# Second layer of a hybrid decoder: retention, state update, recurrence, head norms and small transposes gathered into one block

## Chip, cores and metric

The kernel runs on one core of one Trainium2 chip. The metric is the device time of one execution in microseconds (us); lower is better. Several runs of a kernel are timed, and one execution is recorded by the hardware profiler.

## The reference

One inference step of a two-layer decoder: a prompt of 16 meta and 512 prompt tokens (528 columns here) and eight sequences of four new tokens (32 columns), so T = 560 columns in all. The change lies in the mixer of the second layer, which joins a RetNet retention (four heads of 128) and a gated recurrence (RG-LRU, width 512):

```python
def retention_chunk(S, seqs):
    ...
    intra = jnp.einsum('bhts,bhsv->bhtv', jnp.einsum('bhtd,bhsd->bhts', q, k) * D, v)
    inter = jnp.einsum('bhtd,bhdv->bhtv', q, S) * jnp.exp((t + 1.0)[None, :] * lg[:, None])[None, :, :, None]
    ...
    S_new = jnp.exp(L * lg)[None, :, None, None] * S + jnp.einsum('bhsd,hs,bhsv->bhdv', k, w_src, v)
    return S_new, intra + inter

def mixer_odd(...):
    ...
    mu = jnp.mean(hr, axis=-1, keepdims=True)
    var = jnp.mean(jnp.square(hr - mu), axis=-1, keepdims=True)
    hr = (hr - mu) * lax.rsqrt(var + EPS) * ret_ln_g.astype(f32)[None, :, None, :]
    hr = jax.nn.silu(rg.astype(f32)) * from_heads(hr)
    ...
    r = jax.nn.sigmoid(...)
    ig = jax.nn.sigmoid(...)
    log_a = -LRU_C * r * jax.nn.softplus(-lru_lambda.astype(f32))
    a = jnp.exp(log_a)
    bx = jnp.sqrt(-jnp.expm1(2.0 * log_a)) * (ig * xc)
    bx = bx.at[:, 0].add(a[:, 0] * h0)
    _, hs = lax.associative_scan(_lin_combine, (a, bx), axis=1)
    hl = hs * jax.nn.gelu(lgate.astype(f32))
    out = jnp.concatenate([hr, hl], axis=-1).astype(xn.dtype) @ w_out
    return out, S_new, hs[:, -1], u[:, -(CONV_W - 1):]
```

The new retention states, the last recurrence values and the last three convolution inputs are outputs as well.

## The kernel before

Activations lie transposed, features on the 128 partitions and the 560 columns along the free axis. Each engine has its own queue and runs it strictly in the order in which the kernel writes it; engines meet at semaphores. Code is written in blocks (`nc.Block()`): a block has one section per engine, and at its end all engines meet in a barrier before the next block begins.

The first layer and the second layer's input projection come first. Then the mixer of the second layer runs in four blocks, one after the other, and after them `close_layer(1, ...)` runs the output projection, the norms and the feed-forward network.

Block 1, `decayed_attention` (L1075 on). Four heads with eight tiles each (the list `ALL`; within a head the tiles are 256, 128, 272, 272, 272, 144, 16 and 32 columns wide). TensorE first runs four products of the all-ones tile with itself (`warm(3)`, L460). Then, for tile i, it writes the scores of tile i+1 (L1092) and adds tile i's weighted values to the head's sums (L1116). Between the two VectorE multiplies the scores by the decay table (L1199, "weights" here). A head's last tile also adds the decode sequences' old states (eight products of 4 columns, L1134). ScalarE copies the sums out of PSUM (L1158, L1161), a head at a time. At the start ScalarE also makes the small lambda columns (with GpSimd), then Silu of `rg` and Gelu of `lgate` (L3084, L3085). SyncE loads the old states.

Block 2, `state_update` (L1312 on). VectorE scales the values of each block of keys by its decay (L1334, with a column copy L1336 that only the first layer needs) and spreads the 32 sample rows over eight sequences (L1341, eight instructions a head). TensorE multiplies them by the keys (L1377, L1381); VectorE adds the sums to the decayed states (L1351; L1360, eight instructions a head). Beside it TensorE makes the recurrence's eight gates (L3110), ScalarE their Sigmoid (L3127), then Tanh and Exp (L3132, L3135), GpSimd the product of input gate and input (L3141). At the end VectorE makes 1 - a squared (L3146).

Block 3 (L3186 on). SyncE stores the new states. TensorE sums each head with the all-ones matrix (L3209), VectorE subtracts the mean (L3231), ScalarE squares (L3264), TensorE sums the squares with one column per head (L3200), VectorE takes 1/(var + eps) (L3236, L3239), ScalarE the root (L3268), TensorE spreads the row over the partitions (L3220), VectorE multiplies (L3247) and GpSimd multiplies by the gate (L3277). In the same queues stand the recurrence's decay (L3261), its root (L3266), inputs (L3171), the four sample steps (L3177, L3179), the four scans over the prompt (L3184, one per 128 channels) and the product with Gelu (L3274). Last VectorE gathers the small rows (L3252 to L3256).

Block 4, `transposes` (L485): the small rows are turned by TensorE, copied (L493, L499) and stored by SyncE (L3291 to L3295); the block ends when the stores have landed.

The order of the work around the change is thus the order of the code in each queue; nothing plans it.

## Time and profile before

| | us |
|---|---|
| median of 3 runs (lowest to highest) | 1703.52 (1691.70 to 1703.73) |
| the profiled execution | 1702.52 |
| its span on the core | 1700.9 |
| mean granted TensorE clock of the span | 0.945 of full speed |
| busy, TensorE / VectorE / ScalarE / GpSimd | 1569.6 / 1022.2 / 619.4 / 293.8 |

Times in the trace count from the span's start. The stage that is changed begins at 1111.2 with the first instruction after a barrier and ends at 1229.6 with the output projection's first product. PE is TensorE, DVE VectorE, ACT ScalarE, POOL GpSimd, SPq SyncE's DMA queue.
### The profile page before, as it was taken

The numbers are of one execution on the slowest core, as the hardware profiler recorded it, in microseconds if no ns is written. First come the engines' busy times: TensorE is split into PE (matmuls) and PEld (weight loads), VectorE is DVE, ScalarE is ACT, GpSimd is POOL, SyncE is SP. The second block draws the span as 40 slices with busy tenths as digits, with TensorE's granted clock in tenths as the row PEclk, the third lists the DMA queues.
The fourth block names the chain that finished last, engine by engine and source line by source line (L and its number), as shares of the span: only waits on it lengthen the run. The fifth ranks groups of instructions, "written<-read, shape, count | busy, mean of one in ns | idle before, by whom it ended". The sixth has DMA issues, their size and how long they took to land. (4 is left out here: it accounts for less than half of the span.)

```text
span 1700.9 us, 31137 instructions
## 1 busy us (share of the span) xinstructions
PE 1569.6 (92%) x11877; PEld 1459.3 (86%) x11877; DVE 1022.2 (60%) x1761; ACT 619.4 (36%) x1073; POOL 293.8 (17%) x304
## 2 busy tenths in 40 slices
PE   7999989988889999999999899998498999999996
PEld 5999966766578999999999899975298999999996
DVE  5332454544556988888322867427658988885225
ACT  3111322435334435556122422224234345555221
POOL 2411001300000154443000100001300344441000
PEclk8999987979999999999999999988599999999998
DMA  5232151777351123333332132211130323325311
GB/s 141 78 100 62 50 163 38 230 217 251 96 163 50 50 76 99 99 99 103 92 99 66 50 99 98 87 50 46 49 112 1 99 76 99 99 80 131 93 43 53
DMA packets 225861, 161.15 MB, mean 95 GB/s; under 512 B 17949, under 2 KB 206089, under 8 KB 225760
## 3 DMA queue, kind: packets, MB, share of 16 engines
q1 hardware_dynamic: 222480, 157.94, 32.1%
q0 software_dynamic: 3280, 1.85, 0.5%
q8 instruction: 66, 1.08, 0.3%
q14 instruction: 35, 0.29, 0.1%
HBM read 150.13 MB, written 9.89 MB: 94 GB/s over the span
## 5 line engine op out<-in xcount | busy, mean ns | idle before, releaser
L2315 ACT CAST w_high<-ring 128x1024 fp32r<-128x1024 f32 (+1 forms) x68 | 81.5, 1199 | 345.2 <-PE psum L2045 317.8
L2149 PE MATMUL psum<-t_high,piece_high 128*128 128x280 f32 (+1 forms) x512 | 150.0, 293 | 10.2 <-ACT product L2460 7.5
L2625 DVE TENSOR_TENSOR w_low<-ring,w_high 128x1024 fp32r<-128x1024 f32 (+1 forms) x68 | 96.0, 1412 | 100.2 <-ACT w_high L2315 100.2
L2151 PE MATMUL psum<-t_high,piece_low 128*128 128x280 f32 (+1 forms) x512 | 149.4, 292 | 0.0
L2150 PE MATMUL psum<-t_low,piece_high 128*128 128x280 f32 (+1 forms) x512 | 149.2, 291 | 0.0
L2415 ACT CAST piece_high<-ring 128x512 fp32r<-128x512 f32 x160 | 99.1, 622 | 76.6 <-PE psum L2151 55.0
L2149 PE MATMUL psum<-b_high,piece_high 128*128 128x280 f32 (+1 forms) x384 | 112.5, 293 | 0.0
L2151 PE MATMUL psum<-b_high,piece_low 128*128 128x280 f32 (+1 forms) x384 | 112.4, 293 | 0.0
L2150 PE MATMUL psum<-b_low,piece_high 128*128 128x280 f32 (+1 forms) x384 | 112.2, 292 | 0.0
L2149 PEld LDWEIGHTS psum<-t_high,piece_high 128*128 128x128 f32 x512 | 97.4, 190 | 11.1 <-ACT product L2460 7.9
L2150 PEld LDWEIGHTS psum<-t_low,piece_high 128*128 128x128 f32 x512 | 97.5, 190 | 0.0
L2151 PEld LDWEIGHTS psum<-t_high,piece_low 128*128 128x128 f32 x512 | 97.3, 190 | 0.0
L343 PE MATMUL psum<-normed_high,w_high 128*128 128x280 f32 x448 | 94.3, 292 | 0.6 <-PEq L530 0.6
L2740 DVE TENSOR_TENSOR piece_low<-ring,piece_high 128x512 fp32r<-128x512 f32 x96 | 92.8, 970 | 1.8 <-ACT piece_high L2415 1.6
L343 PE MATMUL psum<-normed_high,w_low 128*128 128x280 f32 x448 | 93.8, 290 | 0.0
L343 PE MATMUL psum<-normed_low,w_high 128*128 128x280 f32 x448 | 93.5, 290 | 0.0
L2045 PE MATMUL psum<-hidden_high_a,w_high 128*128 128x280 f32 (+1 forms) x308 | 89.3, 290 | 0.0
L2045 PE MATMUL psum<-hidden_high_b,w_high 128*128 128x280 f32 (+1 forms) x308 | 89.2, 290 | 0.0
L2045 PE MATMUL psum<-hidden_low_b,w_high 128*128 128x280 f32 (+1 forms) x308 | 89.1, 289 | 0.0
L2045 PE MATMUL psum<-hidden_high_a,w_low 128*128 128x280 f32 (+1 forms) x308 | 89.1, 289 | 0.0
L2045 PE MATMUL psum<-hidden_low_a,w_high 128*128 128x280 f32 (+1 forms) x308 | 89.1, 289 | 0.0
L2045 PE MATMUL psum<-hidden_high_b,w_low 128*128 128x280 f32 (+1 forms) x308 | 89.0, 289 | 0.0
(541 smaller groups left out, 4613.6 us busy)
## 6 DMA issues: line engine op xcount, KB each, us to landing
ring<-in_ffn_wd SPq DMA_DIRECT2D x16, 1408.0 KB, 7.0
ring<-in_ffn_wg SPq DMA_DIRECT2D x40, 512.0 KB, 4.0
ring<-in_ffn_wu SPq DMA_DIRECT2D x40, 512.0 KB, 5.2
ring<-in_w_in_even SPq DMA_DIRECT2D x14, 1024.0 KB, 5.3
ring<-in_w_in_odd SPq DMA_DIRECT2D x12, 1024.0 KB, 5.1
ring<-in_cache_fox_k SPq DMA_DIRECT2D x44, 256.0 KB, 4.2
projected<-in_cache_fox_v SPq DMA_DIRECT2D x28, 256.0 KB, 3.2
projected<-in_cache_fox_k SPq DMA_DIRECT2D x20, 256.0 KB, 4.2
```

Of the source, the lines that this page charges most:

```text
L343: last = nc.tensor.matmul(banks[2 * tl + half][:, 0:HALF], w[:, k, :], m[:, half * HALF:(half + 1) * HALF], start=(kk == 0 and w is w_high ...
L2045: done = mm(banks[2 * tl + a][:, 0:HF], w, m[a], start=first and s == 0, stop=last and s == 2)
L2149: mm(bank, wh[:, k], xh[:, k, :], start=(j in (0, 1, 3) and k == 0), stop=False, skip_group_check=True)
L2150: mm(bank, wh[:, k], xl[:, k, :], start=False, stop=False, skip_group_check=True)
L2151: last = mm(bank, wl[:, k], xh[:, k, :], start=False, stop=(k == 3), skip_group_check=True)
L2315: nc.scalar.copy(dst, src).then_inc(w_hi[p], 1)
L2415: nc.scalar.copy(dst, chunks(src, 4) if j in (0, 1, 5) else src).then_inc(pc_high, 1)
L2625: v.tensor_tensor(dst, src, high_.bitcast(F32), ALU.subtract).then_inc(w_lo[p], 1)
L2740: last = v.tensor_tensor(chunks(pc_l[j][:, :], 4), chunks(src, 4), chunks(pc_h[j][:, :], 4).bitcast(F32), ALU.subtract)
```

## The change

The four blocks become one. Nothing of the first layer changes but the place from which some semaphores are taken (`decode_sem` in place of `sem`, which frees them after the first layer). In the new block:

- The four warm-up products are gone; TensorE begins with the first two gates. Gates 2 to 6 follow tiles 3 to 7, gate 7 tile 9. The transposes of the convolution rows stand after tile 18.
- Each head's weighted sums get their own pair of banks by the parity of the head, so the next head does not wait for the copy.
- Between the tiles' weights VectorE scales the sources of the first two heads, and from tile 18 on does the recurrence: 1 - a squared after tiles 18 to 21, the inputs after 24 to 27, the sample steps after tile 29, scans 0 and 1 after tiles 30 and 31, scans 2 and 3 between the head norms.
- Centring is a product: TensorE multiplies a head by (identity - 1/128) (`centre`). ScalarE squares that product out of PSUM, and VectorE multiplies it by `rg` in one step. `rg` has been through Silu and has been multiplied by the norm's gain on GpSimd. The last step is one product with the spread root.
- The spreading of sample rows is one instruction of 1024 elements per head in place of eight; adding to the states is two of 512 in place of eight of 128; the column copies are gone.
- The final row gathering is on GpSimd. SyncE stores the convolution rows early and the new states when all four heads are updated; the block ends when all stores have landed.

The core of the diff (the loops that set the order; the waits are shown where the prediction speaks of them):

```diff
-    decayed_attention(rq, rk, TK["mv"], Cst, bufs, False, dtab, dsm[:, :, 0:NS],
-                      lambda_by_scalar, lambda_by_gpsimd, None, load_ret_state, s_st2)
-    state_update(TK["mk"], TK["mv"], Cst, lambda n, b, hd: dsm[0:n, hd, 2 * NS + b:2 * NS + b + 1],
...
-    transposes(jobs, store_lru)
+        def _(sp):
+            load_ret_state(sp)
+            sp.wait_ge(rows_copied, 2)
...
+            sp.wait_ge(rows_copied, 4)
...
+            sp.wait_ge(state_done, MH)
+            for b in range(NB):
+                sp.dma_start(io["s_ret_S"][b].rearrange("h k v -> k h v"),
...
+            sp.wait_ge(stored, 16 * 16)
...
+            for i in range(len(ALL)):
+                if i + 1 < len(ALL):
+                    score(i + 1)
+                values(i)
+                if 3 <= i <= 7:
+                    lru_gate(i - 1)
+                if i == 9:
+                    lru_gate(7)
+                if i == 18:
+                    turn_conv()
+                if i == 26:
+                    centred_head(0)
+                if i == 30:
+                    centred_head(1)
+            centred_head(2)
+            update(0)
+            centred_head(3)
+            update(1)
+            for hd in range(MH):
+                variance(hd)
+            update(2)
+            update(3)
+            turn_fin()
+            for hd in range(MH):
+                spread_rstd(hd)
...
+            for c in range(4):
+                nc.scalar.activation(gt[:, c, :], ga[:, c, :], ACT.Tanh, scale=lam[:, 2, c:c + 1]).then_inc(tanh_done, 1)
+            for i in range(2):
+                act.wait_ge(rows_turned, i + 1)
+                n = (3, 24)[i]
+                nc.scalar.copy(crow[i][0:n, :], banks[i][0:n, :]).then_inc(rows_copied, 1)
+            for c in range(4):
+                nc.scalar.activation(hs[:, c, :], ga[:, c, :], ACT.Exp, scale=lam[:, 0, c:c + 1]).then_inc(a2_done, 1)
+            copied(1)
...
+            def one_minus_a2(c):
+                dve.wait_ge(tanh_done, c + 1)
+                dve.wait_ge(a2_done, c + 1)
...
+            def recurrence_input(c):
+                dve.wait_ge(root_done, c + 1)
...
+            for i in range(len(ALL)):
+                weights(i)
+                if i % 8 < 5 and i < 16:
+                    source_block(i // 8, i % 8)
...
+                if 18 <= i < 22:
+                    one_minus_a2(i - 18)
+                if 24 <= i < 28:
+                    recurrence_input(i - 24)
+                if i == 28:
+                    scaled_head(0)
+                if i == 29:
+                    sample_steps()
+                if i >= 30:
+                    scan(i - 30)
+            scaled_head(1)
+            scan(2)
+            scaled_head(2)
+            state(0)
+            scan(3)
+            scaled_head(3)
+            sources(2)
+            state(1)
+            sources(3)
+            dve.wait_ge(variances, MH)
...
+            v.reciprocal(vrow, vrow).then_inc(inverted, 1)
+            state(2)
+            state(3)
```

Three places show how the queues change. The first is TensorE's queue where the stage begins; `ones` is the all-ones tile, `convolved` the gates' input. Before:

```order
L460 MATMUL psum<-ones 128x512 x4
L1092 MATMUL psum<-projected 128x256
L1092 MATMUL psum<-projected 128x128
L1116 MATMUL psum<-projected,token_major_6482 128x256
L1092 MATMUL psum<-projected 128x272
L1116 MATMUL psum<-spare,token_major_6482 128x128
L1092 MATMUL psum<-projected 128x272
L1116 MATMUL psum<-projected,token_major_6482 128x272
```

and after:

```order
L3165 MATMUL psum<-convolved,projected 128x280 x4
L3136 MATMUL psum<-projected 128x256
L3136 MATMUL psum<-projected 128x128
L3148 MATMUL psum<-projected,token_major_6480 128x256
L3136 MATMUL psum<-projected 128x272
L3148 MATMUL psum<-projected,token_major_6480 128x128
L3136 MATMUL psum<-projected 128x272
L3148 MATMUL psum<-projected,token_major_6480 128x272
L3136 MATMUL psum<-projected 128x272
L3148 MATMUL psum<-projected,token_major_6480 128x272
L3165 MATMUL psum<-convolved,projected 128x280 x2
L3136 MATMUL psum<-projected 128x144
```

Two gates (four products of 280 columns) stand where the warm-up stood, and single gates come between tiles from tile 3 on.

The second is ScalarE's queue from the gates' Tanh on (`root` takes it; `rstd` is the row of the norm). Before, in blocks 2 and 3:

```order
L3132 ACTIVATE root<-input_gate,lam 128x560 x4
L3135 ACT_TABLE_LOAD
L3135 ACTIVATE projected<-input_gate,lam 128x560 x4
L1326 UNCONDITIONAL_BRANCH
L3258 UNCONDITIONAL_BRANCH
L3261 ACTIVATE input_gate<-input_gate,lam 128x560 x4
L3264 ACTIVATE token_major_6482<-projected 128x560 x4
L3266 ACT_TABLE_LOAD
L3266 ACTIVATE root<-root 128x560 x4
L3268 ACTIVATE rstd<-rstd 4x560
```

and after:

```order
L3302 ACTIVATE root<-input_gate,lam 128x560 x4
L3306 COPY projected<-psum 3x512
L3306 COPY projected<-psum 24x512
L3308 ACT_TABLE_LOAD
L3308 ACTIVATE recurrent<-input_gate,lam 128x560 x4
L3272 COPY projected<-psum 128x256
L3272 COPY projected<-psum 128x304
L3312 ACTIVATE input_gate<-input_gate,lam 128x560 x4
L3313 ACT_TABLE_LOAD
L3313 ACTIVATE projected<-projected 128x2240
L3316 ACT_TABLE_LOAD
L3316 ACTIVATE root<-root 128x560 x4
```

The copies of the turned convolution rows (L3306) now stand between Tanh and the Exp of a squared; Silu of `rg` (L3313) stands between the decay and the root (L3316).

The third is VectorE's queue in the third head of the retention, tiles 16 on; `decay_table` is the factor of a tile's weights. Before:

```order
L1199 TENSOR_TENSOR projected<-psum,decay_table_6485 128x256
L1199 TENSOR_TENSOR spare<-psum,decay_table_6485 128x128
L1199 TENSOR_TENSOR projected<-psum,decay_table_6485 128x272
L1199 TENSOR_TENSOR spare<-psum,decay_table_6485 128x272
L1199 TENSOR_TENSOR projected<-psum,decay_table_6485 128x272
L1199 TENSOR_TENSOR spare<-psum,decay_table_6485 128x144
L1199 TENSOR_TENSOR projected<-psum,decay_table_6485 16x16
L1199 TENSOR_TENSOR spare<-psum,dsm 32x32
```

and after:

```order
L3340 TENSOR_TENSOR projected<-psum,decay_table_6483 128x256
L3340 TENSOR_TENSOR projected<-psum,decay_table_6483 128x128
L3340 TENSOR_TENSOR projected<-psum,decay_table_6483 128x272
L3372 SCALAR_TENSOR_TENSOR root<-recurrent,root 128x560
L3340 TENSOR_TENSOR projected<-psum,decay_table_6483 128x272
L3372 SCALAR_TENSOR_TENSOR root<-recurrent,root 128x560
L3340 TENSOR_TENSOR projected<-psum,decay_table_6483 128x272
L3372 SCALAR_TENSOR_TENSOR root<-recurrent,root 128x560
L3340 TENSOR_TENSOR projected<-psum,decay_table_6483 128x144
L3372 SCALAR_TENSOR_TENSOR root<-recurrent,root 128x560
```

After tile 18's weights an instruction of the recurrence (L3372, 1 - a squared) follows each tile's weights, ahead of those of the next tile.

## Rows read from the trace of the kernel before

**Rows 1.** Windows: stretch, length, busy PE, PEld, DVE, ACT, POOL, granted clock, DMA share, GB/s.
```profile
1111.10:1116.40 5.30, 5.23 (x9) 2.25 (x10) 0.00 (x0) 5.13 (x7) 1.33 (x6) 0.68 0.71 206
...
1116.40:1152.60 36.20, 35.79 (x193) 28.43 (x191) 10.66 (x32) 7.45 (x11) 0.00 (x0) 0.91 0.10 28
...
1182.90:1219.60 36.70, 18.93 (x48) 9.92 (x48) 25.00 (x48) 9.70 (x14) 13.39 (x8) 0.64 0.23 65
```

**Rows 2.** Timeline, TensorE, retention: start, length, engine, line, what, count.
```profile
1111.17 5.37 PE L460 MATMUL psum<-ones 128*128 128x512 f32 x8 [2.20 <-PEq L124]
...
1116.37 0.82 PE L1092 MATMUL psum<-projected 128*128 128x256 f32 x4
...
1133.28 1.95 PE L1134 MATMUL psum<-qs,states 128*128 128x4 f32 x16
...
1137.76 1.11 PE L1116 MATMUL psum<-projected,token_major 128*128 128x272 f32 x2
...
1142.96 1.95 PE L1134 MATMUL psum<-qs,states 128*128 128x4 f32 x16
...
1150.54 1.95 PE L1134 MATMUL psum<-qs,states 128*128 128x4 f32 x16
```

**Rows 3.** Timeline, TensorE: two gates, four products of 280 columns.
```profile
1162.16 2.15 PE L3110 MATMUL psum<-convolved,projected 128*128 128x280 f32 x8
```

**Rows 4.** Instructions by line, ScalarE, in the stage: busy time, mean ns of one.
```profile
L3132 ACT ACTIVATE root<-input_gate,lam 128x560 f32<-128x560 f32 x4 | 2.7, 750 | 0.1
...
L3135 ACT ACT_TABLE_LOAD x1 | 1.3, 1283 | 0.1
...
L3084 ACT ACTIVATE projected<-projected 128x2240 f32<-128x2240 f32 x1 | 2.1, 2070 | 0.0
...
L3266 ACT ACTIVATE root<-root 128x560 f32<-128x560 f32 x4 | 2.3, 657 | 0.0
...
L1158 ACT COPY projected<-psum 128x256 f32<-128x256 f32 (+1 forms) x6 | 2.3, 389 | 21.9 <-PE psum L1134 18.6 <-PE psum L1116 3.4
```

**Rows 5.** Instructions by line, VectorE, from the state update to the end.
```profile
L3171 DVE TENSOR_TENSOR spare<-spare,root 128x560 f32<-128x560 f32 x4 | 2.6, 707 | 0.0
...
L3184 DVE TENSOR_TENSOR_SCAN recurrent<-input_gate,spare 128x528 f32<-128x528 f32 x4 | 6.9, 1797 | 0.1
...
L3231 DVE SCALAR_TENSOR_TENSOR projected<-psum,projected 128x280 f32<-128x280 f32 x8 | 3.2, 444 | 6.5 <-PE psum L3209 6.5
...
L1360 DVE SCALAR_TENSOR_TENSOR states<-states,psum 128x128 f32<-128x128 f32 x32 | 6.6, 277 | 0.0
...
L3239 DVE RECIPROCAL rstd<-rstd 4x560 f32<-4x560 f32 x1 | 3.6, 3641 | 0.1
...
L3179 DVE TENSOR_TENSOR recurrent<-recurrent,spare 128x32 f32<-128x32 f32 x4 | 0.9, 218 | 0.3
```

**Rows 6.** Timeline, VectorE and GpSimd, with and without each other.
```profile
1154.83 1.65 DVE L1341 TENSOR_SCALAR projected<-token_major,mwbuf 32x128 f32<-32x128 f32 x8
...
1157.99 3.97 DVE L1341 TENSOR_SCALAR projected<-token_major,mwbuf 32x128 f32<-32x128 f32 x8
...
1158.03 1.37 POOL L3141 TENSOR_TENSOR spare<-spare,convolved 128x560 f32<-128x560 f32 x1 [42.37 <-ACT spare L3127]
...
1205.09 8.10 POOL L3274 TENSOR_TENSOR projected<-recurrent,projected 128x560 f32<-128x560 f32 x4 [30.82 <-DVE recurrent L3184]
```

**Rows 7.** Timeline and waits, state stores and entry to the output projection.
```profile
1182.91 5.95 SPq L3190 DMA_DIRECT2D out_s_ret_S<-states  x8
...
1188.90 0.88 SPq L3192 DMA_DIRECT2D out_p_ret_S<-cp  x1
...
SPq L3186 <- DMA out_p_ret_S<-cp: 2.8, 1, 2.8
...
1226.54 0.41 SPq L1972 DMA_DIRECT2D first_w<-in_ffn_wg  x1
...
1229.64 0.79 PE L2045 MATMUL psum<-mixed_high,w_high 128*128 128x272 f32 x2 [7.71 <-DVE mixed_low L2633]
```

More of the change, by code:

```diff
@@ new lines, in hybrid_decoder @@
+    crow = [flat(lx)[0:24, 1024 + 512 * i:1536 + 512 * i] for i in range(2)]
+    vrow = rstd[0:4, :]
+    halves = [slice(0, HALF), slice(HALF, T)]
+    own = smask[:, 32:40]
+    (scored, weighted, weights_used, num_copied, centre_made, centred, scaled, squared, variances, inverted, rooted, spread,
+     head_done) = (sem(x) for x in (
+         "scores", "weights", "weights_used", "num_copied", "centre_matrix", "centred", "centred_scaled", "centred_squared",
+         "variances", "variances_inverted", "rstd_rows", "rstd_spread", "head_done"))
@@ new lines, in centred_head @@
+            def centred_head(hd):
+                if hd == 0:
+                    pe.wait_ge(centre_made, 1)
+                    pe.wait_ge(rows_copied, 2)
+                elif hd == 2:
+                    pe.wait_ge(num_copied, 8)
+                else:
+                    pe.wait_ge(scaled, hd)
+                    pe.wait_ge(squared, hd)
+                pe.wait_ge(num_copied, 2 * hd + 2)
+                for half in range(2):
+                    last = mm(centre_banks(hd)[half][:, 0:HALF], centre, xn[:, hd, halves[half]], start=True, stop=True)
+                last.then_inc(centred, 1)
@@ new lines, in variance, with update @@
+                last.then_inc(variances, 1)
+            def update(hd):
+                pe.wait_ge(sourced, hd + 1)
+                if hd == 0:
+                    pe.wait_ge(scaled, 2)
+                    pe.wait_ge(squared, 2)
+                    pe.wait_ge(weighted, len(ALL))
+                elif hd == 1:
+                    pe.wait_ge(num_copied, 6)
+                else:
+                    pe.wait_ge(state_done, hd - 1)
+                for b in range(SB):
+                    n = BLK[b][1]
+                    mm(sum_bank(hd)[:, 0:128], TK["mk"][0:n, b, hd * 128:(hd + 1) * 128], vw[hd % 2][0:n, b, :],
+                       start=(b == 0), stop=(b == SB - 1))
+                ks = TK["mk"][0:NS, SB, hd * 128:(hd + 1) * 128]
+                for half in range(2):
+                    last = mm(sequence_banks(hd)[half][:, :], ks,
+                              vm[hd % 2][:, 4 * half:4 * half + 4, :].rearrange("p b v -> p (b v)"), start=True, stop=True)
+                last.then_inc(updated, 1)
@@ new lines, in scan, with scaled_head @@
+            def scan(c):
+                v.tensor_tensor_scan(hs[:, c, 0:TP], ga[:, c, 0:TP], gi[:, c, 0:TP], 0.0, ALU.mult, ALU.add).then_inc(scanned, 1)
+            def scaled_head(hd):
+                dve.wait_ge(squared, hd + 1)
+                dve.wait_ge(gain_rg, hd + 1)
+                for half in range(2):
+                    last = v.tensor_tensor(xn[:, hd, halves[half]], centre_banks(hd)[half][:, 0:HALF], rg[:, hd, halves[half]],
+                                           ALU.mult)
+                last.then_inc(scaled, 1)
@@ new lines, in state @@
+            def state(hd):
+                dve.wait_ge(updated, hd + 1)
+                v.tensor_copy(cp[:, hd, 0:128], sum_bank(hd)[:, 0:128])
+                st = states[:, :].rearrange("p (b h v) -> p b h v", b=NB, h=MH)
+                for half in range(2):
+                    x = st[:, 4 * half:4 * half + 4, hd, :]
+                    last = v.scalar_tensor_tensor(out=x, in0=x, scalar=GAMMA4[hd],
+                                                  in1=sequence_banks(hd)[half].rearrange("p (b v) -> p b v", b=4),
+                                                  op0=ALU.mult, op1=ALU.add)
+                last.then_inc(state_done, 1)
@@ L3251, in _ @@
[L3251 to L3268 removed]
+                    c = halves[half]
```

415 lines of the change are left out of this document (233 added, 182 removed).

## Prediction

> **What bounds the kernel now.** I read the windows first, to find a stage in which TensorE is not the limit; then the timeline of that stage engine by engine, for what each engine waits on; then the instructions by line, for prices. The windows show the stage [rows 1]: during the retention (1116.4 to 1152.6) TensorE is busy throughout and VectorE for 10.7 of 36.2 us; in the third block (1182.9 to 1219.6) TensorE is busy for 18.9 of 36.7 us at a mean granted clock of 0.64, and VectorE for 25.0. So the stage has a part in which TensorE works and the others are idle, and a part in which they work in a chain and TensorE waits. It runs from 1111.17, the warm-up products [rows 2], to 1229.64, the first product of the output projection [rows 7]: 118.5 us. Everything before and after is unchanged, so I put the new block's work on the same clock and ask when that first product starts.
>
> **The change, step by step.** Each step follows the engine that is late.
>
> (a) *To the end of the convolution transposes after tile 18* (call it Y): TensorE is late. Before, the first score stood at 1116.37 and tile 18 of the third head ended at 1138.87 (1137.76 + 1.11): 22.5 us for 19 tiles [rows 2]. That now begins 5.2 us earlier, at 1111.17. Added in front of Y are eight gates. Two gates take 2.15 us with the latency of the last product [rows 3], so some 0.95 each: 7.6 us. Eight transposes of 128 columns move 1024 columns; at the rate of [rows 3], about 590 columns per us of fp32 product they take at most 1.7, I take 1.5. The first 5.3 us had a granted clock of 0.68 [rows 1], and useful work now lies in them: 0.32 x 5.3 = 1.7 us lost. Against that the gates fill waits: heads two and three end with the state products 9.7 us apart (1133.28, 1142.96), head four 7.6 us later (1150.54), for the same work [rows 2]. Of these twice 2.1 us I give 2.0 back. Y = 1111.2 + 22.5 + 7.6 + 1.5 + 1.7 - 2.0 = 1142.5. VectorE's scaled sources, which now stand between the tiles, cost 0.21 each at the rate of the first line of [rows 6], one per tile of about 0.9 us or more: hidden by TensorE; not hidden, twelve of them would be 2.5 us.
>
> (b) *From Y to the first root*: ScalarE is late. It stands at the copies of the transposed rows, so its Exp can't begin before Y, although the Tanh is long done; and 1 - a squared, which waits for that Exp, stands in VectorE's queue ahead of tile 19's weights, so TensorE waits for VectorE and VectorE for ScalarE. ScalarE then runs [rows 4]: two copies 0.8, table load 1.28, four Exp 2.7, two copies 0.8, four Exp 2.7, table load 1.28, Silu 2.07, table load 1.28, first root 0.6: 13.5, with handoffs 14.0. First root at 1156.5. TensorE's tiles 19 to 24 are less than this and lie beside it.
>
> (c) *To tile 28's weights*: VectorE is late. Four recurrence inputs 2.6 (L3171 in [rows 5]) and the weights of tiles 25, 26, 27 between them (128 and twice 272 columns; a product of 280 out of PSUM takes 0.40 by L3231, 3.2 over 8): 1.2. 1160.3.
>
> (d) *To the end of the retention* (t0): VectorE again. Weights 28 0.4; head 0's product with `rg` 0.8 (two of L3231's size); weights 29 0.3; eight sample steps at 0.29 (0.22 of L3179 and a drain) 2.3; weights 30 0.2; scan 1.74 (L3184, 6.9 over 4); weights 31 0.2: 5.9, with handoffs 6.3. TensorE ends with a tile and eight state products, 2.3. t0 = 1168.9. Before, this was 1152.5: the retention itself becomes longer, because it takes the others' work into its queues.
>
> (e) *To the last head's states*: ScalarE's copy 0.4 and square 0.9 come first, then VectorE is late: three products with `rg` 2.4, two scans 3.5, four state updates, two sources, the variance row 0.8 (two of 280 columns, as L3231) and the reciprocal 3.64 [rows 5]. A state update was a copy and eight instructions, 6.6 / 4 = 1.65 for the eight; two instructions over the same elements lie between twice the 0.66 of L3171's 560 columns, scaled to 512, that is 1.2, and 1.65; with the copy I take 1.5, four are 6.0. The sources: five scalings and a small one 1.3, and one instruction of 1024 elements, between 1.2 (1024/560 of 0.66) and the 1.65 of the first line of [rows 6]; I take 1.2, since one instruction is nearest the 560-column row; twice 2.5 is 5.0. Sum 21.3, and 0.4 waiting for TensorE's first update. TensorE's own work here, about 17 us at 590 columns per us (four updates of 1664 columns, four variance pairs, two centrings), is shorter and lies beside it. t0 + 23.0 = 1191.9.
>
> (f) *The stores.* The eight state stores wait for the last head; issue to landing was 1182.91 to 1188.90 + 0.88 + 2.8 = 1192.6: 9.7 us [rows 7]. Before, norms and recurrence lay beside them; now only the last norm products (four spread pairs and four products of 0.8) do, and the block's end waits for the stores: 1201.6. The small rows' stores stand ahead of them in SyncE's queue, and end at about the same time as the last state update; if they are late, the stores are late with them.
>
> (g) *Entry*: from the first DMA of the next block to the first product 3.1 us [rows 7], and I allow 0.4 from landing to that DMA: 1205.1.
>
> Saved: 1229.64 - 1205.1 = 24.5 us. From the profiled execution's 1702.52 (its span is 1700.9, 1.6 less; it lies 1.0 under the median of the runs shown) that leaves 1678. What goes by name: the warm-up, three barriers, the third block's chain (Exp, root, inputs, scans one after the other) and the last transposes with their stores; what comes back is a longer retention and stores with nothing left beside them.
>
> Not shown by the trace: GpSimd's product of `rg` with a column. Its nearest row is 1.37 (L3141, same 560 columns, two tiles) and for an operation at the same engine 2.03 at most (8.10 over 4) [rows 6]; it is needed at (d), some 5 us after Silu, and hidden either way.
>
> **A rule against the change.** In [rows 6] eight VectorE scalings take 1.65 alone and 3.97 beside two GpSimd products, 1.16 more for each product. The scans, with two inputs in SBUF, kept 1.74 each, while GpSimd's products beside them rose from 1.37 to 2.03. The Trainium skill, page "SBUF — State Buffer", section "Who interferes with whom", says that a VectorE instruction with two SBUF inputs, or a scaling or copy in a two-port mode, and a GpSimd instruction that reads SBUF exclude each other, and that the one that starts later waits. The trace agrees for the scalings, and in the scans it was GpSimd that lost. By that rule the recurrence inputs of (c) could each be held by a product of `rg` with its gain, 4 x 1.37 = 5.5 us, and the time would be 1683.5; the GpSimd rival below holds that and more.
>
> **Rivals.** *GpSimd holds VectorE.* Twelve GpSimd products stand beside VectorE work that is now on the path (four with the input gate, four with the gain, four with Gelu). At 1.16 us each [rows 6] that is 13.9 us: 1692. For it: VectorE is late in (c) to (e). Against: most products out of PSUM have one SBUF input, and the Gelu products are held back until the last score.
>
> *The clock and the waits are kinder.* If TensorE gets its full clock after the start and the gates fill every wait, Y comes after 19 tiles at head four's pace (19/8 x 7.6 = 18.1), 7.6 gates, 1.0 transposes and 1.7: 1139.6; and with updates and sources at their lower bounds (1.2 less in (e)) the time is 1674.
>
> *The clock stays low; slower than before.* Every wait of TensorE that (b) and (d) introduce is a pause after which it may run at 1.2 GHz, as the third block shows (0.64) [rows 1]. At half clock throughout, (a)'s 28 us of work at full speed (18.1 + 7.6 + 1.5) double and Y comes at 1166, 24 later; in (e) TensorE's 17 us become 34 against VectorE's 23, 11 later: 1713, so 35 lost against 24.5 saved. It decides where the mean granted clock of the block falls under about 0.6; the retention before had 0.91 [rows 1], and its queue was no fuller than the new one. The Trainium skill, page "TensorE: Matmul & The Clock Gate", section "HAM oscillation — how this bites in real kernels", describes that: bursts divided by waits begin throttled each time. By that rule the waits of (b) would bring on this rival in part.
>
> **How the numbers follow.** Forecast 0.55, kinder 0.22, GpSimd 0.18, low clock 0.05. The likeliest gives 1678. The range holds the first three: from 1662 (the kinder case, less the 12 us by which the lowest run before lies under the median) to 1695 (the GpSimd case, with 3 us for its own handoffs). One per cent of 1703.5, about what a measurement can tell from no change, is 17 us, so faster by over 1% means under 1686.5: forecast (0.53 of 0.55), kinder, and little of the GpSimd case (0.03): 0.78. Within 1%: the rest of these and most of the low-clock case: 0.19. Slower by over 1%: 0.03.
>
> **What would show it.** In the new trace: the first gate at the block's start and no warm-up; the first wait of (b), VectorE idle after tile 18's weights for ScalarE's Exp, some 3 us, and again before the first input for the root; VectorE's weights 28 to 31 spread over 6 us; the retention's last product near 1169; state stores issued near 1192 with SyncE's last wait on them; the output projection's first product near 1205. Wrong would be: a granted clock under 0.7 between tiles 19 and 31; VectorE scalings or inputs of twice their length beside GpSimd; stores issued well before the last norm product of 0.8 us has run, with the end set by the norms; or a time outside the stage that moves.

## The result, and the profile after

The changed kernel takes 1678.8 us, the median of four runs (1674.0 to 1684.1), against 1703.6 for the kernel before (1691.7 to 1705.1): a ratio of 0.988, with a 95% interval of 0.985 to 0.992, which is some 20 us; the medians themselves lie 24.8 us apart. Timed once more beside other runs it took 1680.2 against 1703.4, a ratio of 0.986 (0.982 to 0.990). The profiled execution took 1684.14 us, the longest of the first four.

Whole times move by 5 us and more from one execution to the next, largely ahead of the stage: in the fourteen profiled executions of this study, whose programs are the same up to there, the stage began anywhere from 1102.7 to 1115.9 us. Behind the stage thirteen of them took 469.7 to 472.2 us, and one, the run with the warm-up put back, 467.1. So below, the stage itself is what is compared, from its first product to the output projection's first product, each time in the clock of its own trace. It was 118.5 us before [rows 2, 7]. After, in TensorE's timeline (start, length, line, names, shape, count, and the idle time before):

```profile
1112.40 2.89 PE L3165 MATMUL psum<-convolved,projected 128*128 128x280 f32 x8 [2.03 <-PEq L124]
...
1211.59 0.79 PE L2045 MATMUL psum<-mixed_high,w_high 128*128 128x272 f32 x2 [7.67 <-DVE mixed_low L2633]
```

1211.59 - 1112.40 = 99.2 us: the stage is 19.3 us shorter, where 24.5 had been forecast. Its windows, cut at the points of the prediction's steps (transposes after tile 18, first root, end of the retention, last state); the columns are those of [rows 1], the number behind POOL being the granted clock:

```profile
1112.30:1145.20 32.90, 32.62 (x151) 25.77 (x152) 12.32 (x34) 15.11 (x29) 8.59 (x18) 0.84 0.24 64
1145.20:1158.50 13.30, 9.78 (x36) 7.28 (x35) 4.46 (x10) 13.13 (x18) 1.79 (x2) 0.60 0.02 5
1158.50:1174.70 16.20, 14.14 (x56) 11.20 (x55) 9.89 (x23) 6.65 (x11) 9.17 (x7) 0.71 0.00 1
1174.70:1198.40 23.70, 21.85 (x86) 12.28 (x86) 19.92 (x38) 4.67 (x11) 3.21 (x5) 0.92 0.01 1
1198.40:1211.60 13.20, 5.50 (x13) 3.51 (x13) 5.17 (x11) 3.10 (x5) 0.00 (x0) 0.52 0.78 219
```

Two things stand there. TensorE is busy in the first stretch for 32.6 of 32.9 us and in the fourth for 21.9 of 23.7: what lay behind the retention does lie beside it now. Over the whole stage, before and after:

```profile
1111.10:1229.60 118.50, 85.18 (x346) 56.15 (x346) 65.60 (x201) 41.53 (x64) 20.32 (x18) 0.78 0.15 43
```
```profile
1112.30:1211.60 99.30, 83.90 (x339) 60.05 (x339) 51.76 (x115) 42.66 (x71) 22.76 (x31) 0.76 0.19 51
```

TensorE's busy time and clock are nearly the same; its waiting fell from 33.3 to 15.4 us, which is 17.9 of the 19.3 us saved.

The second thing is the granted clock, 0.91 in the retention before [rows 1]. It is 0.84, then 0.60 and 0.71, between the clock's two levels. In the first stretch it is low at the start and again ahead of the end of the transposes, and there TensorE is busy without a break:

```profile
1112.30:1116.70 4.40, 4.21 (x13) 3.10 (x13) 0.81 (x3) 4.21 (x6) 1.15 (x6) 0.65 0.69 201
...
1138.00:1145.20 7.20, 7.20 (x29) 5.87 (x29) 0.73 (x2) 0.42 (x1) 0.00 (x0) 0.56 0.00 0
```

ScalarE's timeline shows who is late after tile 18, and VectorE's who waits for it:

```profile
1132.90 2.72 ACT L3302 ACTIVATE root<-input_gate,lam 128x560 f32<-128x560 f32 x4
1144.78 1.05 ACT L3306 COPY projected<-psum 3x512 f32<-3x512 f32 x2 [9.16 <-PE psum L3174]
...
1147.14 2.72 ACT L3308 ACTIVATE recurrent<-input_gate,lam 128x560 f32<-128x560 f32 x4
...
1157.92 2.35 ACT L3316 ACTIVATE root<-root 128x560 f32<-128x560 f32 x4
```
```profile
1148.01 0.74 DVE L3372 SCALAR_TENSOR_TENSOR root<-recurrent,root 128x560 f32<-128x560 f32 x1 [5.62 <-ACT recurrent L3308]
...
1158.62 1.08 DVE L3378 TENSOR_TENSOR spare<-spare,root 128x560 f32<-128x560 f32 x1 [3.46 <-ACT root L3316]
...
1167.88 1.24 DVE L3393 TENSOR_TENSOR_SCAN recurrent<-input_gate,spare 128x528 f32<-128x528 f32 x1
```

ScalarE has its Tanh done at 1135.6 (1132.90 + 2.72) and stands for 9.16 us at the copies of the turned rows, L3306, until TensorE has turned them; the Exp, L3308, comes after. VectorE waits 5.62 us for that Exp and 3.46 for the first root, the two waits that the prediction named (the first as some 3 us). At the end, SyncE's queue:

```profile
1198.40 5.96 SPq L3122 DMA_DIRECT2D out_s_ret_S<-states  x8
...
1208.48 0.38 SPq L1972 DMA_DIRECT2D first_w<-in_ffn_wg  x1
```

The stores go out as the last state is done, and the next block's first DMA follows 10.1 us after their first issue, long after the last norm product (1203.96 + 0.80, VectorE).

This table is worked out from the traces, as microseconds after the stage's first product. "First root" is the start of the first Sqrt; for the forecast that is its first root at 45.3 less the 0.6 that the root takes.

| kernel | transposes end | first root | retention ends | last state | next block's product | median, us |
|---|---|---|---|---|---|---|
| forecast | 31.3 | 44.7 | 57.7 | 80.7 | 93.9 | 1678 |
| changed | 32.8 | 45.5 | 62.3 | 86.0 | 99.2 | 1678.8 |
| changed, again | 32.8 | 45.5 | 62.3 | 86.0 | 99.2 | 1680.2 |
| a1 Exp first | 32.8 | 38.1 | 54.3 | 78.5 | 91.7 | 1675.7 |
| a2 warm-up back | 33.6 | 46.4 | 62.8 | 93.1 | 107.2 | 1682.5 |
| a3 stores by head | 32.8 | 45.5 | 62.3 | 86.0 | 95.7 | 1680.2 |
| a4 gain left out | 33.1 | 45.8 | 62.7 | 86.4 | 99.6 | (1678.6, one run) |
| a5 gates first | 40.0 | 52.7 | 68.8 | 92.7 | 106.0 | 1689.5 |
| a6 unread products | 33.1 | 45.8 | 59.3 | 83.0 | 96.2 | (1685.3, one run) |
| a7 = a1 and a3 | 33.1 | 38.5 | 54.7 | 78.8 | 89.6 | 1668.7 |
| a8 = a7 and products | 29.9 | 36.5 | 50.8 | 76.6 | 86.8 | 1669.0 |

The ratios to the kernel before, with their intervals: a1 0.986 (0.979 to 0.993), a2 0.988 (0.982 to 0.995), a3 0.989 (0.982 to 0.995), a5 0.992 (0.989 to 0.996), a7 0.982 (0.978 to 0.986), a8 0.979 (0.975 to 0.982). The intervals of a1, a2, a3 and a5, and at its edge that of a7, overlap the changed kernel's, so by whole times they can't be told from it with certainty; what is read below from the stages rests on one execution each. Of the six runs of a8 each is faster than every one of the changed kernel timed beside them (1664.4 to 1671.1 against 1676.8 to 1684.6).

### The profile page after: what moved, and what is told of

Its sections match the earlier page's. It is cut to its first block and busy times, and to the rows that moved or that the text cites. A ratio compares the mean times of both kernels' runs of the same rounds, so it can differ in the third digit from the quotient of the medians.

```text
span 1682.5 us, 31038 instructions
## 1 busy us (share of the span) xinstructions
PE 1570.8 (93%) x11869; PEld 1464.0 (87%) x11869; DVE 1009.5 (60%) x1675; ACT 620.4 (37%) x1080; POOL 297.5 (18%) x317
```

## The experiments

**The same kernel again**, with no edit.

> The changed kernel once more, with nothing edited. Theory (the stage repeats itself, and the spread of the whole time comes from the clock in the first layer, ahead of the stage): transposes 32.8 to 33.1, end of the retention 62.3, last state 86.0 and first product of the output projection 99.2 after the first gate, each within 1 us, whatever the whole time is. Rival (the clock varies in the stage itself, as in the run with the warm-up, where the part after the retention took 30.3 instead of 23.7): the stage lies anywhere from 96 to 106.

All five points came back to within 0.1 us, though the whole time of that execution was 1678.4 instead of 1684.1. Its stretches, cut as above, show the same clock too:

```profile
1139.60:1152.90 13.30, 9.77 (x36) 7.30 (x34) 4.46 (x10) 13.13 (x18) 1.82 (x2) 0.59 0.02 5
1152.90:1169.10 16.20, 14.13 (x56) 11.19 (x55) 9.91 (x23) 6.62 (x11) 9.14 (x7) 0.71 0.00 1
1169.10:1192.80 23.70, 21.83 (x86) 12.26 (x86) 19.92 (x38) 4.67 (x11) 3.20 (x5) 0.92 0.01 1
```

So the low clock in it is no accident of one execution. But the stage does not repeat in every one: of the eight traces in which TensorE's work up to the transposes is the same, seven end them at 32.8 to 33.1 us and one, the last experiment's, at 29.9, at another clock. A difference of a microsecond may be read from one trace here where it lies in the step that the edit touches; one that comes with another clock elsewhere may be that of one execution.

**ScalarE's copies behind the Exps.**

```diff
-            for i in range(2):
-                act.wait_ge(rows_turned, i + 1)
...
             for c in range(4):
                 nc.scalar.activation(ga[:, c, :], ga[:, c, :], ACT.Exp, scale=lam[:, 3, c:c + 1]).then_inc(a_done, 1)
+            for i in range(2):
+                act.wait_ge(rows_turned, i + 1)
+                n = (3, 24)[i]
+                nc.scalar.copy(crow[i][0:n, :], banks[i][0:n, :]).then_inc(rows_copied, 1)
```

> The changed kernel, with ScalarE's two copies of the turned convolution rows moved behind both sets of Exp. Theory (ScalarE is late from the transposes to the first root, because it stands at these copies from 1135.6 to 1144.8 with its Tanh done): the Exp of a squared runs right after the Tanh, VectorE's wait of 5.6 us for it and its wait of 3.5 us for the root go, and the stage from the first gate to the first product of the output projection falls from 99.2 to 92 to 94 us. Rival (TensorE is late there: it is busy 9.8 of these 13.3 us at a granted clock of 0.60): the waits go over to TensorE's products, and the stage falls by 0 to 3.5 us.

The stage is 91.7 us, 7.5 less, a little more than the theory had. The transposes end at the same 32.8, so all of it comes from step (b) and stays to the end. The trace of this run, TensorE and then ScalarE:

```profile
1106.69 2.90 PE L3165 MATMUL psum<-convolved,projected 128*128 128x280 f32 x8 [2.03 <-PEq L124]
...
1143.33 1.95 PE L3154 MATMUL psum<-qs,states 128*128 128x4 f32 x16
...
1198.42 0.79 PE L2045 MATMUL psum<-mixed_high,w_high 128*128 128x272 f32 x2 [6.66 <-DVE mixed_low L2633]
```
```profile
1131.22 2.72 ACT L3304 ACTIVATE recurrent<-input_gate,lam 128x560 f32<-128x560 f32 x4
...
1144.81 2.35 ACT L3316 ACTIVATE root<-root 128x560 f32<-128x560 f32 x4
```

The Exp now follows the Tanh, and the root comes 5.4 us after the transposes (1139.46) instead of 12.7. TensorE's tiles 19 to 24 keep up with that: they have no wait ahead of them and run at full clock, and head three's state products take 1.95 us at 1143.33 against 3.58 in the changed kernel. The rival had read TensorE's 9.8 busy microseconds as work that had to be done there; it was work at the low clock, with waits around it.

**The warm-up put back** (`warm(3)` ahead of the first gate).

> The changed kernel, with the four warm-up products back ahead of the first gate. Theory (the warm-up cost 5.4 us, and the real work that took its place lost 1.7 of them to the low clock): the first gate comes 5.4 us later and runs at full clock, the stage from the first of these products to the output projection is 99.2 + 3.4 to 5.0. Rival (what the warm-up saved was lost again to a low clock in the first gates and tiles): 99 to 100.5.

Neither. The stage is 107.2, 8.0 longer, but not for the reason given: with 5.2 us of warm-up ahead, the transposes end only 0.8 later. The windows tell why, and where the rest went:

```profile
1121.10:1149.60 28.50, 28.05 (x152) 22.05 (x151) 12.09 (x33) 10.77 (x23) 6.54 (x8) 1.00 0.12 32
...
1178.80:1209.10 30.30, 29.72 (x86) 15.54 (x86) 19.92 (x38) 4.78 (x11) 3.21 (x5) 0.66 0.00 0
```

Behind the warm-up TensorE has its full clock up to the transposes (1.00), where the changed kernel has 0.84: so leaving the warm-up out saved 5.2 us and gave back 4.4 of them here (32.8 against 28.4 from the first gate). In the last experiment below, also without warm-up, that part took 29.9 at 0.94, so what is given back differs between executions. The other 7 us are lost from the end of the retention to the last state, 30.3 us against 23.7, at a clock of 0.66 against 0.92, with TensorE busy for 29.7 of them. What sets the clock low in that stretch is open: TensorE was not waiting there. Nor is it shown to be the edit's doing: the profiled execution was the longest of the four (1691.8; the others 1678.4 to 1683.0), and their median lies only 2 to 4 us above the changed kernel's.

**The kernel before without its warm-up** (`warm(3)` in the first layer's retention only), one part of the change alone.

> The kernel before, without the four warm-up products ahead of the second layer's retention: one part of the change alone. Prediction's price (5.4 us, of which 1.7 are lost to the low clock): the stage of 118.5 falls to 114.5 to 115.5. Rival (by the run with the warm-up put back, in which the transposes came only 0.8 us later, the low clock takes nearly all of it back): 117 to 118.5.

```profile
1112.83 0.89 PE L1092 MATMUL psum<-projected 128*128 128x256 f32 x4 [2.20 <-PEq L124]
...
1228.14 0.79 PE L2046 MATMUL psum<-mixed_high,w_high 128*128 128x272 f32 x2 [7.72 <-DVE mixed_low L2634]
```

1228.14 - 1112.83 = 115.3: 3.2 us less, by the prediction's price. The median was 1699.1 against 1701.05 (ratio 0.999, 0.996 to 1.002), so by time alone it can't be told from nothing.

**The kernel before with the wider update instructions**, the other part that can be had alone. The short form of the edit, for the second layer:

```diff
-                    for b in range(NB):
-                        last = v.tensor_scalar(vm[hd % 2][:, b, :], ..., mw[:, b:b + 1], None, ALU.mult)
+                    last = v.tensor_tensor(vm[hd % 2][:, :, :], ..., mw.unsqueeze(2).to_broadcast([NS, NB, 128]), ALU.mult)
...
-                    for b in range(NB):
-                        s = state[:, b * MH + hd, :]
+                    for half in range(2):
+                        x = st[:, 4 * half:4 * half + 4, hd, :]
```

> The kernel before with the state update's wider instructions alone: one instead of eight for the scaled samples, two instead of eight for a head's states, and no copies of the weights. VectorE is busy for 27.0 of the second block's 30.3 us [rows 5 have its parts]. Theory (VectorE is late there, and what it loses is gained): 4 x 0.44 + 4 x 0.38 from the two lines alone and the copies, 1.4 twice, and the 3.97 of the scalings beside GpSimd: 5 to 7.5 us, a stage of 111 to 113.5. Rival (TensorE, busy for 22.9 of the 30.3, or ScalarE's gates are late next): 1 to 4 us, 114.5 to 117.5.

Below both: the stage is 119.3 (1105.99 to 1225.25), no shorter than before. VectorE's lines in the second block:

```profile
L1346 DVE TENSOR_TENSOR projected<-token_major,mwbuf 32x1024 f32<-32x1024 f32 x4 | 4.9, 1213 | 0.3
...
L1357 DVE COPY cp<-psum 128x128 f32<-128x128 f32 x4 | 1.2, 292 | 12.4 <-PE psum L1394 12.4
```

The scaled samples of a head take 1.21 us, as the prediction's bound had it, and VectorE's busy time in the block falls from 27.0 to 17.9. All of it comes back as 12.4 us of waiting for TensorE's update products (L1357), which stand in one queue with the gates, and these wait for ScalarE (0.97 us at a time). TensorE's clock in the block was 0.85, against 0.90 before, which may be part of why nothing was gained. In the old order shorter instructions were worth nothing; what they are worth in the new one no run shows. So of the 19.3 us the warm-up is some 3 (in the kernel before) and the wider instructions alone nothing; what is left, some 16, is the order of the work together with what was not tried alone: the centring as a product, the dropped barriers, and the wider instructions in the new order. That is by difference and not by a run of its own.

**All gates ahead of the first score.**

```diff
-            lru_gate(0)
-            lru_gate(1)
+            for i in range(8):
+                lru_gate(i)
```

> The changed kernel, with all eight gates ahead of the first score instead of between the tiles. Theory (the gates between the tiles fill waits of TensorE, which the prediction put at 2.0 us): the transposes after tile 18 come 2 us later and the stage is 100.5 to 101.5. Rival (TensorE has no such waits where the gates stand, or ScalarE's earlier Tanh gives them back): 98.5 to 99.5.

The direction is the theory's, the size is not: the transposes end 7.2 us later, the stage is 106.0. TensorE waits 3.38 us for ScalarE's first Sigmoid, which stands behind three table loads and the logarithm of lambda, and gets its eight gates done only at 1130.0, 15.8 us after the first:

```profile
1114.21 2.12 PE L3165 MATMUL psum<-convolved,projected 128*128 128x280 f32 x8 [2.03 <-PEq L124]
1119.72 8.15 PE L3165 MATMUL psum<-convolved,projected 128*128 128x280 f32 x20 [3.38 <-ACT input_gate L3275]
1128.84 1.21 PE L3165 MATMUL psum<-convolved,projected 128*128 128x280 f32 x4 [0.97 <-ACT input_gate L3275]
```

So the gates between the tiles hide ScalarE's pace. The theory's gaps of TensorE's own were not there (see step (a) below).

**Four unread products in each of TensorE's two waits.**

```diff
+                if i in (19, 30):
...
+                    for _ in range(4):
+                        mm(banks[0][:, 0:256], ones[:, :], ones[:, :].unsqueeze(1).to_broadcast([128, 2, 128]), start=True, stop=True)
                 values(i)
```

> The changed kernel with four products of 256 columns, whose results nobody reads, in each of TensorE's two waits of the retention (before tile 19's and tile 30's values). Theory (TensorE's waits bring the low clock on): the state products of heads three and four take 1.95 us each as they do at full clock instead of 3.58, the centring of head 1 some 1.1 instead of 2.2, the granted clock from the transposes to the end of the retention rises from 0.60 and 0.71 to over 0.85, and the stage falls from 99.2 to 95 to 97. Rival (the low clock comes whatever TensorE does there, as in the run with the warm-up, where it stood at 0.66 through 30 us of busy TensorE): these durations stay, and the stage is 99 to 100.

Half of each. The stage is 96.2, inside the theory's range, and all 3.0 us are gained between the first root and the end of the retention, where the clock is 0.87; from the transposes to the first root it is 0.74, and nothing is gained:

```profile
1157.41 3.58 PE L3154 MATMUL psum<-qs,states 128*128 128x4 f32 x16
...
1168.90 1.99 PE L3250 MATMUL psum<-ones 128*128 128x256 f32 x8
...
1172.76 1.95 PE L3154 MATMUL psum<-qs,states 128*128 128x4 f32 x16
```

After the second wait was filled, head four's state products take 1.95 us, at full clock; so they do in the last experiment, and in none of the traces without these products. After the first, head three's still take 3.58: the tile right behind it ran at full clock (0.73 us at 1152.46), the 256-column score at 1155.69 did not (1.22 against 0.70). That wait was filled in part only: 1.29 us of it were left behind the unread products.

**Stores head by head.**

```diff
-            sp.wait_ge(state_done, MH)
-            for b in range(NB):
-                sp.dma_start(io["s_ret_S"][b].rearrange("h k v -> k h v"), ...)
+            for hd in range(MH):
+                sp.wait_ge(state_done, hd + 1)
+                sp.dma_start(io["s_ret_S"][:, hd].rearrange("b k v -> k b v"), by_head[:, hd]).then_inc(stored, 16)
+                sp.dma_start(io["p_ret_S"][0, hd], cp[:, hd, 0:128]).then_inc(stored, 16)
```

> The changed kernel, with the states stored head by head as each is done, instead of sequence by sequence after the last. Theory (the 10.1 us from the last state to the next block's first DMA are the stores alone, with nothing beside them): the last head's store lands some 4 to 5 us after the last state, the block then ends with the last norm products (1204.8), and the stage falls from 99.2 to some 95.5 to 96.5. Rival (a store has a long fixed part from issue to landing, or the earlier stores slow the states or are slower in this shape): 98 to 100.

95.7, as the theory had it, with every point up to the last state where it was:

```profile
1197.29 0.39 SPq L3119 DMA_DIRECT2D out_s_ret_S<-states  x1
1197.72 0.58 SPq L3120 DMA_DIRECT2D out_p_ret_S<-cp  x1
1201.78 0.39 SPq L1972 DMA_DIRECT2D first_w<-in_ffn_wg  x1
```

The next block's DMA follows 4.5 us after the last head's store, 0.3 after the last norm product.

**GpSimd's gain left out.**

> The changed kernel with GpSimd's four products of the gate with the head gain cut to 8 of 560 columns (the rest of the gain is left out). Theory (GpSimd's products lengthen the four recurrence inputs beside them by 0.8 us in all, from 0.66 each to 1.08, 0.72, 0.73 and 0.92, and nothing more): these take 0.66 to 0.73 each and the stage is 98 to 98.8. Rival (each input is held by a product, 1.37 each, as the page's rule had it): 93 to 95.

```profile
1152.69 0.74 DVE L3378 TENSOR_TENSOR spare<-spare,root 128x560 f32<-128x560 f32 x1 [3.46 <-ACT root L3316]
...
1155.62 0.73 DVE L3378 TENSOR_TENSOR spare<-spare,root 128x560 f32<-128x560 f32 x1
```

The four inputs fall to 0.73 each, 2.9 in all instead of 3.45, and the stage doesn't change (99.6). From the first input to tile 28's weights it is 5.4 us, as in the changed kernel (5.3): VectorE now waits 0.82 and 0.72 us for the scores instead, the first of which TensorE gives at the low clock, while the second stands behind head 0's centring in its queue. The gain's products cost nothing there.

**The kernel before with GpSimd held back until the scans are done** (its wait for scan c + 1 made a wait for all four).

> The kernel before, with GpSimd's four products of the recurrence held back until all four scans are done. Theory (VectorE's scans were lengthened by the GpSimd products beside them, as 1.74 before against 1.24 in the changed kernel says): each scan takes 1.24, the four 5.0 instead of 6.9, and GpSimd's products fall from 2.03 to about 1.4. Rival (the prediction's reading, that it was GpSimd alone that lost): scans stay at 1.74.

```profile
1199.39 4.70 DVE L3184 TENSOR_TENSOR_SCAN recurrent<-input_gate,spare 128x528 f32<-128x528 f32 x4
```
```profile
1204.17 5.34 POOL L3274 TENSOR_TENSOR projected<-recurrent,projected 128x560 f32<-128x560 f32 x4 [34.56 <-DVE recurrent L3184]
```

Four scans in 4.7 instead of 6.9 [rows 5], four products in 5.3 instead of 8.1 [rows 6]: both had lost. It is a test of these durations only; the stage, with the products now behind the scans, got no shorter (120.2).

**Both gains together.**

> The changed kernel with both edits: ScalarE's copies behind the Exps, and the states stored head by head. Theory (the two lie one behind the other on the path, the first before the last state and the second after it): the stage is 91.7 less the 3.5 that the stores gave, some 88 to 89 us, and the time lies some 10 us under that of the changed kernel at the same clock in the first layer. Rival (with the states earlier, another wait takes over: the norm products or the clock): 90 to 92.

89.6, between the two: 9.6 of the 11.0 us that the edits gave one by one. The next DMA now leaves at 1189.20, right after the last norm product (1188.93), so the norm products are late in place of the stores, as the rival said.

**And the unread products with them.**

> The changed kernel with ScalarE's copies behind the Exps, the stores by head, and four unread products of 256 columns in TensorE's wait before tile 30's values (that wait alone: the other is gone with the first edit). Theory (the wait before tile 30 brings on the low clock for the end of the retention): the head's state products take 1.95 instead of 3.58 and the stage falls from 89.6 to 86.5 to 87.5. Rival (what the end of the retention gains is lost again behind it to VectorE or to the clock): 89 to 90.5.

86.8, and head four's state products do take the theory's 1.95 us, but the time was not gained by its path. The first stretch, which this edit doesn't touch, is 3.2 us shorter (29.9 instead of 33.1), at another clock:

```profile
1110.80:1140.70 29.90, 29.60 (x151) 23.30 (x152) 13.82 (x37) 21.00 (x38) 8.52 (x18) 0.94 0.26 71
...
1147.30:1161.60 14.30, 14.17 (x62) 10.50 (x61) 9.87 (x23) 7.22 (x11) 8.84 (x7) 0.81 0.00 1
1161.60:1187.40 25.80, 25.30 (x87) 13.83 (x86) 19.63 (x37) 4.78 (x11) 4.60 (x7) 0.79 0.19 54
```

From the transposes to the first root 1.3 us are lost (6.6 against 5.3), from there to the end of the retention 1.9 gained (14.3 against 16.3), and then 1.7 lost up to the last state (25.8 against 24.1, at 0.79 against 0.85) and 0.5 gained behind it. So the unread products' own gain is not shown to last. The time is that of the two edits alone as far as the measurement can tell (1669.0, 1668.7). Both medians lie some 10 us under the changed kernel's.

## Why the prediction was right, and where it was not

The time came out within 1 us of the forecast of 1678, inside the range, and by the medians faster by over 1% (the interval of the ratio reaches to 0.8%). The stage did not: it saved 19.3 us of the 24.5 forecast. The medians differ by 24.8, the two profiled executions by 18.4; the place of the stage in the trace moves by up to 13 us from run to run, so the 5 us between medians and stage need no cause in the kernel, and none is shown. The hit on the time is in part luck. Step by step, with the forecast ahead of the measured length:

- (a) 31.3, 32.8. TensorE is late there and busy throughout, as said. "Against that the gates fill waits", the 2.0 us given back, failed: there was no wait to fill. In the kernel before, heads two and four between the ends of their state products:

```profile
1125.55:1135.23 9.68, 9.68 (x49) 7.73 (x50) 2.69 (x8) 0.79 (x2) 0.00 (x0) 0.82 0.00 0
...
1144.91:1152.49 7.58, 7.58 (x47) 6.07 (x46) 2.26 (x7) 0.79 (x2) 0.00 (x0) 1.00 0.00 0
```

  TensorE is busy for all of both, so the 2.1 us that head two took longer are low clock (0.82 against 1.00) and not waiting; [rows 1] had it busy for 35.79 of 36.20 us. The 22.5 us for 19 tiles were themselves taken at 0.86 (1116.40 to 1138.87), so some 3.1 of them, as an estimate, are low clock (22.5 x 0.14). Without these and without the 2.0, the sum at full clock is 19.4 + 7.6 + 1.5 = 28.5; the run with the warm-up took 28.4 at 1.00. The 1.7 us for the start were right in size (4.4 us at 0.65, so 1.5 lost). Missing was a term for the second spell of low clock, 7.2 us at 0.56, so some 3.2 lost. These errors cancelled in part, and the step is 1.5 us off.
- (b) 14.0, 13.3. Right, both waits in their places; the run with the Exps first shows that ScalarE's standing at the turned rows was the reason, and that 7.5 us go with it.
- (c) 3.8, 5.4. "VectorE is late" failed. It waits 0.64 for a score that TensorE computes at half clock and 0.45 for one that stands behind head 0's centring in TensorE's queue; with the gain's products out of the way its inputs are shorter (2.9 instead of 3.45), it waits longer, and the end is the same.
- (d) 8.6, 10.75. The part up to tile 30's weights was 4.0, as added up. Behind them the prediction had VectorE late with a scan of 1.74 and left out that the centring of head 1 stands in TensorE's queue ahead of tile 31's values. What ran from there was TensorE at the low clock:

```profile
1168.01 0.43 PE L3148 MATMUL psum<-projected,token_major 16*128 16x16 f32 x2 [1.97 <-DVE projected L3340]
1168.36 2.23 PE L3189 MATMUL psum<-projected,spare 128*128 128x280 f32 x4
1170.53 0.63 PE L3148 MATMUL psum<-projected,token_major 32*128 32x32 f32 x2
1171.09 3.58 PE L3154 MATMUL psum<-qs,states 128*128 128x4 f32 x16
```

  6.7 us from the first to the end of the last, against the 1.1 and 1.95 that centring and state products take at full clock. The scans beside it took 1.24.
- (e) 23.0, 23.7. The sum held: the update's two instructions and copy take 1.5, as forecast, the scaled samples 1.21 (1.2), the scans 1.0 us less in all, and VectorE waits 2.06 us for the first update instead of 0.4.
- (f), (g) 13.2, 13.2. Right, and the stores by head show that nothing else held the end.

So the sum missed the stage by 1.5 - 0.7 + 1.6 + 2.1 + 0.7 + 0 = 5.2 us. Most of it fits the clock: the runs show (a) at 28.4 us with a clock of 1.00, and, with the second wait filled, 13.5 us from the first root to the end of the retention at 0.87, instead of 16.75 at 0.71. The prediction's own sign of failure, a granted clock under 0.7 between tiles 19 and 31, did appear:

```profile
1145.20:1174.70 29.50, 23.92 (x90) 18.48 (x89) 14.35 (x33) 19.78 (x27) 10.96 (x8) 0.66 0.01 2
```

0.66 there, though 0.76 in the whole stage. That rival was priced as a low clock throughout (1713) with a chance of 0.05 (its "28 us of work" add up to 27.2, which its 1166 does use); what came was a part of it, and a price for the part was missing. The Trainium skill, page "TensorE: Matmul & The Clock Gate", section "HAM oscillation — how this bites in real kernels", says that bursts of matmuls divided by waits begin throttled each time. The wait before tile 30 agrees with it: behind it head four's state products take 3.58 us, and 1.95 in the two runs that filled it. The wait before tile 19 neither bears it out nor refutes it, since its filling was partial and head three's took 3.58 all the same; and the 7.2 us at 0.56 ahead of the transposes, like the 30.3 us at 0.66 in the run with the warm-up, are no case of it, because TensorE was busy through both. What brings the low clock there is open.

The GpSimd rival fell: the time is not near its 1692, and taking the gain's products away changed nothing. (The gate's and the Gelu's products were not taken away.) But the sentence that "in the scans it was GpSimd that lost" was wrong. With GpSimd's products held back the scans take 1.24 on average instead of 1.80, so VectorE lost over 0.5 us on each as well; the scans' 1.74 was a price with contention in it. In the kernel before:

```profile
1203.75 6.95 DVE L3184 TENSOR_TENSOR_SCAN recurrent<-input_gate,spare 128x528 f32<-128x528 f32 x4
```

The rule of the Trainium skill, page "SBUF — State Buffer", section "Who interferes with whom", that two such instructions exclude each other, fits that better than the prediction's reading. Together the scans and products had taken 9.4 us (1203.75 to 1205.09 + 8.10); one behind the other they take 10.1 (1199.39 to 1204.17 + 5.34), so running them beside each other saved only 0.7.

## What to carry to other kernels

When work is gathered into one block, look in each engine's queue for an early instruction that waits for a late one: here two small copies stood ahead of four Exps, and moving them was worth 7.5 us, more than a third of what the whole change had brought to the stage. Before a piece of work that took longer than its like is said to have waited, look at the engine's busy time and its granted clock there: the 2.1 us a head that were to be filled were low clock at full business. A price taken from a trace holds only with the neighbours and the clock that it had there: ask of each row what ran beside it, and price TensorE's work, behind a wait above all, at the low clock as well as at the high one. Transfers at the end of a block should start as their parts are done.

## What had not been expected of the hardware

- Leaving out 5.2 us of warm-up gave 4.4 of them back, up to the transposes, in the changed kernel's traces (1.5 in one other), and 2.0 in the kernel before (its stage fell by 3.2), where 0.55 is a wait for the load of the old states.
- TensorE's clock can be low while it is busy: 7.2 us without a break at 0.56, in the changed kernel, and in one execution 30.3 us at 0.66 with TensorE busy for 29.7; the same products took 23.7 us at 0.92.
- A scan of 528 columns takes 1.24 us alone and 1.80 beside GpSimd's products; GpSimd's product takes 1.33 (5.34 / 4) alone and 2.03 beside the scans. Both engines lose.
